# The end of a gated MLP on one NeuronCore: the order of the last products, the last convolutions and the residuals, and an early weight split

## The reference, cut to what matters

```
x = x + g1 * (y @ w_out)
h = rmsnorm(x, norm2) * (1 + sc2) + sh2
u = conv3(h @ w_up, conv_ff)          # 1024 -> 2 * 2816 columns, a convolution of width 3 over the tokens
ua, ub = split(u, 2)
x = x + g2 * ((silu(ua) * ub) @ w_down)   # 2816 -> 1024
```

## Time and profile before

| | |
|---|---|
| median of 3 runs | 1819.02 us (1817.84 to 1819.35) |
| the profiled execution | 1815.29 us, its span from first to last instruction 1813.5 us |
| mean granted TensorE clock | 0.969 of full speed |
| busy: PE / DVE / ACT / POOL | 93% / 57% / 33% / 29% of the span |

### The profile page before, as it was taken

One profiled execution on the slowest core, in us unless ns is written; L12 is line 12 of the kernel. 1 busy time (PEld: TensorE's weight loads), 2 busy tenths in 40 slices (PEclk: granted clock), 3 DMA queues, 4 the chain that ended last, 5 costly groups with the idle time before them and its releaser, 6 DMA issues.

```text
span 1813.5 us, 29689 instructions
## 1 busy us (share of the span) xinstructions
PE 1678.7 (93%) x11702; PEld 1516.1 (84%) x11702; DVE 1037.9 (57%) x1647; ACT 603.1 (33%) x1109; POOL 532.2 (29%) x297
## 2 busy tenths in 40 slices
PE   6999998988999999998789999899799999999966
PEld 4887555888999999998768955569699999999966
DVE  4284445237666666666534644532676666666655
ACT  3423444325222232222242244542432222222223
POOL 1354010222333334333125500113133333333320
PEclk8999999999999999999889999999899999999988
DMA  8323540121222222222343154202122222222211
GB/s 314 103 70 113 163 140 13 47 59 47 71 80 71 69 81 69 75 77 93 134 136 93 59 164 147 71 25 74 31 71 73 79 77 74 78 73 69 70 35 59
DMA packets 147729, 156.17 MB, mean 86 GB/s; under 512 B 8200, under 2 KB 118324, under 8 KB 147636
## 3 DMA queue, kind: packets, MB, share of 16 engines
q1 hardware_dynamic: 147636, 154.87, 27.5%
HBM read 151.54 MB, written 3.31 MB: 85 GB/s over the span
## 4 chain that ended last, share of the span: by engine, by line
PE 61%; issue 20%; POOL 9%; ACT 4%; DVE 3%; DMA 1%; POOLq 0%; ACTq 0%; SPq 0%; DVEq 0%
PE PS L1142 56%; POOL W_lo L839 8%; PE PS L1146 5%; ACT HF L913 1%; ACT PT L885 1%; POOL SS L855 1%; DMA AS<-in_w_ada_dram 1%; ACT PR L1019 1%; DVE X L1678 0%; DMA BS_N<-in_w_ada_dram 0%; ACT W_hi L885 0%; ACT H_hi L885 0%; DMA XIN<-in_x_sample_dram 0%; DVE H_lo L1652 0%; ACT PMM L885 0%
## 5 line engine op out<-in xcount | busy, mean ns | idle before, releaser
L839 POOL TENSOR_TENSOR W_lo<-RW,W_hi 128x1024 fp32r<-128x1024 f32 (+1 forms) x184 | 471.8, 2569 | 989.5 <-ACT W_hi L885 989.5
L1142 PE MATMUL PS<-H_hi,W_hi 128*128 128x384 f32 x1856 | 578.6, 312 | 18.9 <-DVE H_lo L1652 7.9
L1142 PE MATMUL PS<-H_hi,W_lo 128*128 128x384 f32 x1856 | 579.0, 312 | 0.0
L1142 PE MATMUL PS<-H_lo,W_hi 128*128 128x384 f32 x1856 | 578.7, 312 | 0.0
L1142 PEld LDWEIGHTS PS<-H_hi,W_hi 128*128 128x128 f32 x1856 | 354.2, 191 | 20.6 <-issue 13.5
L1142 PEld LDWEIGHTS PS<-H_lo,W_hi 128*128 128x128 f32 x1856 | 352.8, 190 | 0.1
L1142 PEld LDWEIGHTS PS<-H_hi,W_lo 128*128 128x128 f32 x1856 | 352.7, 190 | 0.0
L1142 PE MATMUL PS<-G_hi,W_hi 128*128 128x384 f32 x704 | 220.4, 313 | 34.0 <-DVE G_lo L1925 34.0
L885 ACT ACTIVATE W_hi<-RW 128x1024 fp32r<-128x1024 f32 (+1 forms) x184 | 191.2, 1046 | 128.1 <-PE PS L1142 128.1
L1142 PE MATMUL PS<-G_lo,W_hi 128*128 128x384 f32 x704 | 219.6, 312 | 0.0
L1142 PE MATMUL PS<-G_hi,W_lo 128*128 128x384 f32 x704 | 219.3, 311 | 0.0
(11 more groups left out here) (188 smaller groups left out, 1942.7 us busy)
## 6 DMA issues: line engine op xcount, KB each, us to landing
RW<-in_w_up_dram SPq DMA_DIRECT2D x88, 512.0 KB, 3.7
RW<-in_w_ada_dram SPq DMA_DIRECT2D x64, 512.0 KB, 4.0
RW<-in_w_down_dram SPq DMA_DIRECT2D x44, 512.0 KB, 3.6
RW<-in_w_in_dram SPq DMA_DIRECT2D x28, 512.0 KB, 3.7
AS<-in_w_ada_dram SPq DMA_DIRECT2D x16, 512.0 KB, 11.5
RW<-in_w_out_dram SPq DMA_DIRECT2D x32, 128.0 KB, 2.8
RW<-in_w_out_dram SPq DMA_DIRECT2D x8, 512.0 KB, 3.4
BS_N<-in_w_ada_dram SPq DMA_DIRECT2D x8, 512.0 KB, 7.7
```

Of the source, the lines that this page charges most:

```text
L839: nc.gpsimd.tensor_tensor(W_lo[:, slot, 0:width], RW[:, raw, 0:width], W_hi[:, slot, 0:width].bitcast(F32), ALU.subtract).then_inc(w_lo, 1)
L1142: return nc.tensor.matmul(out, lhsT, rhs, start=start, stop=stop, skip_group_check=True)
```

## The change

Five edits, all in a layer's second half:

1. PE's last group waits for 20 blocks of G (pair 9's) instead of 22, works pair 9's q = 0 tile, then pair 10's q = 0 tile with the input block kc as the outer loop: all four output blocks with kc = 0 after the 21st G_lo, all four with kc = 1 after the 22nd.
2. DVE's order in the last pair becomes: convolution 0, residuals 0 and 1, convolution 1, residuals 2 and 3, first gate, convolution 2, first G_lo, residuals 4 to 7, convolution 3, second gate, second G_lo.
3. `silu` of every pair waits for the gate half's convolution alone, where it waited for the value half's too.
4. ACT splits the third up tile inside the norm, behind `modulate` of block 4.
5. The splits that follow move up by one place: the fourth tile's behind the first copy of an up result, the fifth's behind the second; none behind the third.

```
@@ ScalarE
                 for t in range(KT):
                     modulate(l * 2 + 1, 1, t)
+                    if t == 4:
+                        item(l, NPROJ + NOUT + 2)
...
                 def silu(i, ch):
-                    act.wait_ge(cv_done, l * 44 + i * 4 + (2 * ch + 2))
+                    act.wait_ge(cv_done, l * 44 + i * 4 + (2 * ch + 1))
...
                     up_out(0, e, l * NW + (SPL + s0 + e + 1), True)
-                    item(l, s0 + e + 2)
+                    if e != 2:
+                        item(l, s0 + {0: 3, 1: 4, 3: 5}[e])
@@ TensorE
-                pe.wait_ge(g_lo, l * 22 + 22)
-                for p in range(2):
-                    s = NW - 4 + p
-                    pe.wait_ge(w_lo, l * NW + (RAW + s + 1))
+                pe.wait_ge(g_lo, l * 22 + 20)
+                pe.wait_ge(w_lo, l * NW + (RAW + NW - 3))
+                for t in range(4):
+                    pe.wait_ge(up_ev, l * 44 + (40 + t + 1))
+                    for kc in range(2):
+                        ins = gated_product(t, wslot(l, NW - 4), PAIRS % 2, kc, kc == 0, False)
+                ins.then_inc(w_used, 1)
+                pe.wait_ge(w_lo, l * NW + (RAW + NW - 2))
+                for kc in range(2):
+                    pe.wait_ge(g_lo, l * 22 + 21 + kc)
                     for t in range(4):
-                        if p == 0:
-                            pe.wait_ge(up_ev, l * 44 + (40 + t + 1))
-                        ins = gated_products(t, wslot(l, s), (PAIRS - 2 + p) % 2, p == 0, p == 1)
-                        if p == 1 and t < 3:
+                        ins = gated_product(t, wslot(l, NW - 3), (PAIRS - 1) % 2, kc, False, kc == 1)
+                        if kc == 1 and t < 3:
                             ins.then_inc(dn_mm, 1)
-                    ins.then_inc(w_used, 1)
+                ins.then_inc(w_used, 1)
@@ VectorE, dve_pair
+                    if last:
+                        conv_i(0, 0)
+                        dve.wait_ge(dn_add, (l + 1) * NDN + 8)
+                        residual(l, 0)
+                        residual(l, 1)
+                        conv_i(0, 1)
+                        residual(l, 2)
+                        residual(l, 3)
+                        gate(i, 0)
+                        conv_i(1, 0)
+                        g_low(i, 0, (1 + b_) % 2)
+                        for t in range(4, KT):
+                            residual(l, t)
+                        conv_i(1, 1)
+                        gate(i, 1)
+                        g_low(i, 1, (1 + b_) % 2)
+                        return
```

More of the change, by code:

```diff
@@ L1502, in first_items, with gated_product @@
                                 ins.then_inc(w_used, 1)
+                def gated_product(t, slot, gslot, kc, first, last):
+                    return three(halves(t), slot, 512 * kc + P * t, (G_hi[:, gslot, kc, :], G_lo[:, gslot, kc, :]),
+                                 first, last)
                 def gated_products(t, slot, gslot, first, last):
                     for kc in range(2):
-                        ins = three(halves(t), slot, 512 * kc + P * t, (G_hi[:, gslot, kc, :], G_lo[:, gslot, kc, :]),
-                                    first and kc == 0, last and kc == 1)
+                        ins = gated_product(t, slot, gslot, kc, first and kc == 0, last and kc == 1)
                     return ins
@@ L1963, in add_i @@
                     def add_i(q):
[L1964 to L1971, removed]
+                        down_add(q, l * NDM + i * 6 + (3 * q - 6), l * NW + m * 12 + (SPL + s0 + 6 * b_ + 5 + q),
+                                 l * NDN + i * 8 + 4 * q)
+                    if last:
[15 more added lines that the diff above has]
+                        return
                     conv_i(0, 0)
```

## The result

The changed kernel takes **1773.05 us** (median of 4 runs, 1772.28 to 1773.33); the kernel before, run beside it, 1818.43 us (1817.74 to 1819.35). The ratio is 0.9749, 95% interval 0.9733 to 0.9766: 45.4 us less. The forecast was 1775.3, faster, range 1770 to 1787. The profiled execution of after took 1772.28 us with a span of 1770.4 us, against 1815.29 and 1813.5; by the spans 43.1 us are gone, where the sum of the prediction was 43.7.

What follows compares the result with a forecast made beforehand. PE, busy 93% of the span, was taken as the bound, so only its stops could pay: 17.4 + 18.0 (last groups) + 3.6 + 4.7 (third up tile) = 43.7 us, from 1819.0 to 1775.3 us, range 1770 to 1787.

Steps and rivals of the forecast that it cites:

- The last group: Last four tiles of each layer: PE's 17.0 us wait for G_lo shrinks to 1.2, gaining 17.4 and 18.0 us.
- PE's steps: Last group: pair 9's tile from 855.64, half of pair 10's to 866.28, 1.2 us wait, end at 885.2.
- the end without POOL: First layer's last pair: the 22nd G_lo at 863.1 us if POOL cost DVE nothing, against 867.5 forecast.
- Rival (a): Last pair: POOL keeps DVE out for both W_lo, PE waits 3.6 us a layer; 6.9 us less gain, 1782 us; 10%.
- The residuals: DVE's last pair: residuals 0 to 3 fit the waits of 2.63 and 2.66 us before convolutions 1 and 2, costing nothing.
- The third up tile: Both layers: W_lo moved into the norm removes PE's 3.34 us stop, gaining 3.6 and 4.7 us.
- 1.1 us to spare: Second layer's norm: last H_lo needed by PE at 1306.5, ready at 1305.4; 0.4 us of the split's cost exposed.
- (c): Layer's end: the next layer's modulation rows land late; at 5 us beyond, 1780 us; 4%.
- (b): Norm pays for the third tile: all 1.45 us exposed in both layers, 4.5 us less gain, 1780 us; 6%.
- (e): Last group: PE's first product still waits for W_lo or a PSUM bank; only the third tile gains, 1811 us; 2%.
- (d): All 20 full pairs: edit 3 sets W_lo against convolution 3, DVE loses 2.7 us each, 54 us in all; 1829 us; 2%.

Runs made afterwards that it cites:

- the kernel with the W_lo behind G: Changed kernel, but in the last pair ACT rounds G_hi before splitting the next-to-last down tile, PE waiting for the two last W_lo singly: 1770.78 us, ratio 0.9735.
- the third tile alone: Kernel before with edits 4 and 5 alone (third up tile split inside the norm, later splits one place up): 1809.47 us, ratio 0.9954.
- the early silu alone: Kernel before with edit 3 alone (silu waits for its own half's convolution): 1819.31 us, ratio 1.0004.
- The four parts measured alone: Kernel before with edits 4 and 5, edit 1, edit 2, or edit 3: 1809.47, 1794.01, 1809.33 and 1819.31 us.
- PE's order alone: Kernel before with edit 1 alone (last group begins with pair 9's tile, kc outer for pair 10's): 1794.01 us, ratio 0.9868.

## Why the prediction was right

**The last group.** PE's steps held, each within 0.3 us. PE starts right behind the last up tile; the 22nd G_lo ends 11.8 us behind that (852.17 to 863.97), where the prediction had 11.9 (855.64 to 867.5); PE waits 1.10 us, predicted 1.2. What was a little short is the length without a wait: 28.49 us in the kernel that has none, where four tiles of 7.09 were taken; and a wait of 1.10 us costs 1.36, by the difference of the two kernels (the third up tile's stop of 3.34 us in the first layer likewise cost 3.6). Together that is the 0.3 us by which the gain is smaller in each layer.

**POOL against DVE.** The delay came out right and its place wrong. Against the end without POOL, 863.1 in the prediction, it added 4.4 us, in the residuals and the first tap. In the trace the residuals and the first tap are free, and the second and third tap are held up 2.0 us each, 4.05 in all. The first W_lo did not hold up a residual; by the estimate in the last section it was held up itself, by the residuals and the first tap. That the sum came out is in part luck: in either account two W_lo hold up one operation of DVE each, and which ones was told wrong. The prediction's claim that one operation of DVE gets in between the two W_lo is what the ends of the rows say: second tap 858.45, second W_lo 860.71, third tap 861.40. Rival (a), in which none gets in, did not occur. The rule of the Trainium skill, SBUF — State Buffer, section "SBUF: two separate sides", that an operation of VectorE with two SBUF inputs and one of GpSimd shut each other out for their whole length, agrees with these rows: taps of 2.91 and 2.92 us in after and 0.89 in the kernel with the W_lo behind G, and G_lo of 2.39 and 0.82 us. It also agrees in the other direction, a W_lo of 4.90 us beside residuals, which the prediction did not weigh. Who gets the turn between two operations set the place of the delay, and that was not foreseen.

**The residuals** in the waits of DVE cost nothing, as said: 0.77 us of wait is left ahead of convolution 1. The early silu is worth 0.3 us a layer at the tail, and nothing that the times show in the other pairs.

**The third up tile.** The stop of 3.34 us is gone in both layers. The split costs the norm 1.30 us, predicted 1.45. What of that PE sees was forecast as 0 and 0.4 us. In both layers the stretch up to the first up result is 0.6 us longer than before (16.02 against 15.41, 15.49 against 14.88), but most of it is the clock and not the split. In the first layer the clock is at 0.83 against 0.86, and a kernel with no split there takes 16.16 us at 0.83. In the second it is at 0.87 against 0.90: PE's products fall to their full-speed length 4.24 us behind the first one (1276.26, first row), before 3.09 us behind it (1295.60, second row), and PE has no wait for H_lo. The product that takes up the last H_lo (done at 1286.28) takes 0.44 us instead of 0.34 (third row); the split itself shows as some 0.1 us.

```profile
1276.26 0.28 PE L1145 MATMUL PS<-H_hi,W_hi 128*128 128x256 f32 x1
```

```profile
1295.60 0.29 PE L1142 MATMUL PS<-H_hi,W_lo 128*128 128x256 f32 x1
```

```profile
1286.33 0.44 PE L1145 MATMUL PS<-H_hi,W_hi 128*128 128x384 f32 x1
```

With the clock back as early as before, PE would have waited for that H_lo, and the stretch would have been 15.5 us too, as in the third tile alone. So the term was 0.6 us at an early clock, where 0.4 was forecast, and 0.1 as it came. It was sized too small because PE, before, took up that block at 1306.31, 0.86 us behind the last H_lo (done at 1305.45), where the prediction counted 1.1 us to spare. That the layer's gain, 4.5 us, is so close to the 4.7 is in part luck. By two profiles alone the clock's share would have passed for a cost of the norm. The gain of the third tile itself in the first layer is 3.01 + 0.61 = 3.6 us, as predicted.

**The other rivals.** (c), late modulation rows: SP starts the last five at 864.85, with the 22nd G_lo and the residuals done, and PE's waits for BS_N are 2.8 us in all, 3.0 before, so the rows are not later for PE than they were.

```profile
864.85 2.75 SPq L698 DMA_DIRECT2D BS_N<-in_w_ada_dram  x5
```

(b) and (e) fall with the third tile alone and the rows of PE; (d) with the early silu alone.

**The sum.** 17.2 + 17.7 + 3.0 + 4.5 = 42.4 us at the four edges, of the 43.7 predicted there; 0.7 us in the rest of the span, spread over the start and the stretches between, were not predicted. The four parts measured alone give 9.1 + 24.5 + 9.2 - 0.8 = 42.0 us, all together 45.4, and 44.7 when the changed kernel was run again (1819.49 to 1774.81); with intervals of up to 3 us either way on each this is no sign that they help each other.

## What to carry to other kernels

Where the busiest engine waits for the last of many results, first look for work that needs only the earlier ones, and put it ahead of the wait (24.5 us here, without one operation made faster); only then shorten the chain behind the wait (9.2 us alone). Work that is moved into another engine's idle time is free as long as that engine still waits behind it; read that wait off the trace (2.63 us before, 0.77 after). And when VectorE's last step decides, see which GpSimd operation an edit lets loose beside it: a split behind the step instead of beside it was worth 1.36 us a layer.

## What was not expected of the hardware

- The same two weight tiles, with no wait, took 14.83 to 16.31 us behind the same 3.94 us stop, with a granted clock of 0.90 to 0.81 over the stretch. What makes the clock come back early or late there is open; it moves a stage by 1.5 us, more than some of the edits.
- Which of VectorE and GpSimd loses is not fixed: two W_lo took 6.55 us beside residuals and taps in after, one took 4.90 us beside residuals with PE's order alone, and 2.91 us beside residuals in the kernel before, where DVE lost 2.1 us. What decides it is open.
- The first tap, a TENSOR_SCALAR with one tensor as input, took 0.55 us in the last pair of after, inside the record of a W_lo, though 1.44 beside one in the earlier trace rows. A W_lo's record can hold a wait of its own. The single W_lo of the kernel with the split behind G took 3.51 us instead of 2.40; counted back 2.40 from its end (858.18), its work began at some 855.8, when the first tap there (855.38, 0.55 us) was nearly done. By this estimate the first tap had its turn ahead of that W_lo.
